# A four-layer fp32 block on one core: nine weight slots and one used once, layers that open with the high part of x, and other waits at their openings

## What is computed

```python
x = x + rmsnorm(even_mixer(rmsnorm(x)))   # attention of 16 heads beside a state-space model
x = x + rmsnorm(odd_mixer(rmsnorm(x)))    # pooling at four scales, gates, two projections
for layer in range(2):
    h = h + hybrid_mixer(rms_norm(h))     # retention of 4 heads beside a gated recurrence of 4 heads
    h = h + expert_choice_ffn(rms_norm(h))
# expert_choice_ffn: softmax over 16 experts; each expert takes its 32 best tokens (top_k),
# silu(xe @ w_gate) * (xe @ w_up) @ w_down, all [1024, 1024], scattered back with the gates
return rms_norm(h)
```

## Time and profile before

| | |
|---|---|
| three runs | 1701.05, 1702.65, 1705.38 us, median 1702.65 |
| the profiled execution | 1701.89 us, its span 1700.1 us |
| PE, PEld busy | 1330.2 us (78%), 931.5 us (55%) |
| DVE, ACT, POOL busy | 558.6, 433.6, 139.2 us |
| transfers | 517.22 MB, 304 GB/s over the span |
| the chain that ended last | 45% transfers, 39% PE, 6% DVE, 3% SP's queue |

### The profile page before, as it was taken

How to read it: one execution, slowest core, us unless ns; L and a number is a source line. 1 busy time by engine, 2 the same in 40 slices (tenths; PEclk the granted TensorE clock), 3 DMA queues, 4 the chain that set the end, 5 groups by cost and what they waited for, 6 DMA issues and landing times.

```text
span 1700.1 us, 28164 instructions
## 1 busy us (share of the span) xinstructions
PE 1330.2 (78%) x12488; PEld 931.5 (55%) x12488; DVE 558.6 (33%) x804; ACT 433.6 (26%) x570; POOL 139.2 (8%) x155
## 2 busy tenths in 40 slices
PE   7999989999899987656556665999977666666564
PEld 5688867998798844323222322788843333233232
DVE  7854775455566530000000001485520000000001
ACT  5236335443554311100101001454311101001011
POOL 0130300000304000000000000304000000000000
PEclk9999999999999979888888888999989878879887
DMA  9134333464444699999999999344799999999996
GB/s 327 51 120 154 112 136 143 154 221 171 142 156 174 255 387 425 424 426 423 426 424 425 425 425 411 125 149 174 301 403 423 426 424 425 425 423 426 423 425 263
DMA packets 86216, 517.22 MB, mean 304 GB/s; under 512 B 6352, under 2 KB 6480, under 8 KB 53072
## 3 DMA queue, kind: packets, MB, share of 16 engines
q1 hardware_dynamic: 82592, 509.20, 73.8%
q0 software_dynamic: 992, 3.42, 0.6%
q10 hardware_dynamic: 2512, 2.75, 0.5%
HBM read 514.30 MB, written 1.05 MB: 303 GB/s over the span
## 4 chain that ended last, share of the span: by engine, by line
DMA 45%; PE 39%; DVE 6%; SPq 3%; POOL 2%; ACT 2%; issue 2%; DVEq 0%; ACTq 0%; POOLq 0%
DMA ring<-in_w_down 15%; DMA ring<-in_w_up 14%; PE dense L1562 8%; PE dense L1564 8%; PE dense L1563 8%; DMA ring<-in_w_gate 7%; DMA board<-in_w_up 5%; PE bank L2073 3%; SPq L608 3%; DMA board<-in_w_down 2%; PE dense L1579 2%; DMA ring<-in_even_w_in 2%; PE bank L2098 1%; DVE ring_parts L1211 1%; ACT ring_parts L832 1%
## 5 line engine op out<-in xcount | busy, mean ns | idle before, releaser
L2073 PE MATMUL bank<-ring,board 128*32 128x256 f32 x2432 | 194.7, 474 | 144.0 <-DMA ring<-in_w_up 68.1
L2073 PEld LDWEIGHTS bank<-ring,board 128*32 128x32 f32 x2432 | 90.6, 131 | 242.1 <-DMA ring<-in_w_up 84.8
L1211 DVE TENSOR_TENSOR ring_parts<-ring,ring_parts 128x4096 fp32r<-128x4096 f32 (+1 forms) x44 | 183.8, 4187 | 110.7 <-ACT ring_parts L832 110.6
L1004 ACT ACTIVATE board<-bank 128x256 f32<-128x256 f32 x32 | 12.3, 384 | 751.9 <-PE bank L2073 751.9
L1482 DVE TENSOR_TENSOR board<-board,bank 128x256 f32<-128x256 f32 x32 | 13.5, 422 | 562.2 <-ACT board L1004 562.2
L832 ACT ACTIVATE ring_parts<-ring 128x4096 fp32r<-128x4096 f32 (+1 forms) x45 | 154.1, 3432 | 100.8 <-DMA ring<-in_w_in 43.9
L2073 PE MATMUL bank<-board 128*32 128x256 f32 x1664 | 118.9, 435 | 67.7 <-DMA board<-in_w_up 46.1
L1562 PE MATMUL dense<-board_parts,ring_parts 128*128 128x256 f32 x528 | 152.2, 288 | 3.1 <-DVE ring_parts L1211 3.1
L1562 PE MATMUL dense<-ring_parts,board_parts 128*128 128x512 f32 x352 | 143.3, 407 | 8.5 <-ACT board L757 2.3
L1564 PE MATMUL dense<-board_parts,ring_parts 128*128 128x256 f32 x528 | 149.4, 283 | 0.0
L1563 PE MATMUL dense<-ring_parts,board_parts 128*128 128x512 f32 x352 | 138.8, 394 | 0.0
(11 more groups left out here) (330 smaller groups left out, 2036.5 us busy)
## 6 DMA issues: line engine op xcount, KB each, us to landing
ring<-in_w_gate SPq DMA_DIRECT2D x38, 2048.0 KB, 42.0
ring<-in_w_up SPq DMA_DIRECT2D x38, 2048.0 KB, 42.1
ring<-in_w_down SPq DMA_DIRECT2D x38, 2048.0 KB, 41.6
board<-in_w_gate SPq DMA_DIRECT2D x26, 2048.0 KB, 42.4
board<-in_w_up SPq DMA_DIRECT2D x26, 2048.0 KB, 41.0
board<-in_w_down SPq DMA_DIRECT2D x26, 2048.0 KB, 42.1
ring<-in_w_in SPq DMA_DIRECT2D x18, 2048.0 KB, 8.0
ring<-in_even_w_in SPq DMA_DIRECT2D x10, 2048.0 KB, 10.3
```

The source lines that it names most:

```text
L1211: tt(lo, slot_of(u), hi.bitcast(F32), ALU.subtract).then_inc(lo_done, 1)
L2073: last = mm(WB[0][32 * q:32 * q + 32, 256 * (j % 2):256 * (j % 2) + 256], xeT[:, 4 * (j // 2) + k, :], w[:, k * D + 256 * q:k * D + 256 * ...
```

## The change

Line numbers here and in the lists are those of the changed kernel where a list says so.

1. **Slots.** Expert units turn through nine slots. The tenth (`ONCE`) takes unit 9 of each expert layer and nothing more. The experts' loop has a head of two (`HEAD_E`), four turns of three, and two behind it. The loads of the first ten units of a layer wait for what they waited for before.
2. **High parts of 11, 12, 13** are made by ACT, between the exponentials, not by POOL.
3. **Openings of layers 2 and 3** (`opening_unit`): for each tile, PE issues high x times both parts of w as soon as each half of high x is there, then waits for low x and issues its products, then transposes the second tile. The parts of the second unit (`SECOND`, 15 and 31) are made in halves (ACT, `high_half`) and quarters (DVE) inside `norm_between`.
4. **Opening of layer 4**: PE waits for x by halves (`full_half`); DVE makes the low part of unit 138 before it multiplies the second tile by the gain.
5. **Waits**: `ret_transposes(w)` waits for its own four rotations; the first output unit waits for `DO + 10`, takes tile 1 first and waits for `DO + 11` in its middle.
6. **Zero matmuls**: 128x512 zeros; one round of four as before, and three rounds more (twelve matmuls) behind the affinities' transposes. DVE writes the zeros later.
7. **Ends**: the last expert unit of a layer comes in four transfers of 512 KB, awaited one by one; the last scatter goes by accumulators and releases DVE's first addition after four of eight; the output is scaled and sent in halves, four transfers of 256 KB.

```diff
-WHEEL = RING + EXTRA
-TURN_E = 5
-
-EXTRA_OF = {2: 2, 3: 1, 4: 0, 9: 3}
+WHEEL = RING + EXTRA - 1
+TURN_E = 3
+
+
+ONCE = WHEEL
+HEAD_E = 2
+EXTRA_OF = {2: 2, 3: 1, 4: 0}
+
+
+def wheel_place(j):
+
+    return j if j < ONCE else (j - ONCE - 1) % WHEEL
+
+
+def extra_slot(j):
+
+    return EXTRA - 1 if j == ONCE else EXTRA_OF.get(wheel_place(j))
...
-                    elif j >= WHEEL:
-                        sp.wait_ge(unit_done, u - WHEEL + 1)
+                    elif j > ONCE:
+                        sp.wait_ge(unit_done, u - (WHEEL if j - ONCE > WHEEL else WHEEL + 1) + 1)
...
+                    elif turn is None and e == NE - 1 and j == 5:
+
+                        for n in range(4):
+                            src = down[e, :, 2 + n // 2, n % 2, :]
+                            dst = slot_mem(s)[:, n * FF:(n + 1) * FF]
+                            sp.dma_start(dst, src).then_inc(tail_in[n - 1] if n else landed[s], 16)
+                        return
                     else:
...
                 sum_rms(0)
                 dense_rms(1)
                 gain_high(0, at)
+                high_half(SECOND[k - 1], 0)
                 sum_rms(1)
+                high_half(SECOND[k - 1], 1)
...
+            def high_half(u, half):
+
+                if half == 0:
+                    act.wait_ge(landed[slot_no[u]], 16 * count_in[u])
+                    act.wait_ge(unit_done, free_at(high_place[u]))
+                k = slice(4 * half, 4 * half + 4)
+                s.activation(slot_of(u, True)[0][:, k], slot_of(u)[:, k], ACT.Copy).then_inc((hi_half, hi_done)[half], 1)
...
             exps(3)
             t_out(9, gaT, 0, ACT.Silu)
+            high_part(11)
             exps(4)
             t_out(10, gaT, 4, ACT.Silu)
-            for n in (5, 6, 7):
-                exps(n)
+            high_part(12)
+            exps(5)
+            exps(6)
+            high_part(13)
+            exps(7)
             high_part(14)
             norm_between(13, 1)
-            high_part(15)
             for g in range(4):
                 high_part(16 + g)
                 tok_out(14 + g, u_tok, 512 * g)
...
                         tt(x[:, i, half], x[:, i, half], xs[:, i, half], ALU.add).then_inc((sum_half, x_ready)[b], 1)
+                    if i:
+                        low_part(SECOND[k - 1], 0)
                     dve.wait_ge(x_ready, 2 * (k - 1) + i + 1)
                     dve.wait_ge(sum_half, 2 * (k - 1) + i + 1)
                     normalise(i)
+                    if i:
+                        low_part(SECOND[k - 1], 1)
                     gain_out(i, name, x_lo if k == 1 else x_lo2)
+                low_part(SECOND[k - 1], 2)
+                low_part(SECOND[k - 1], 3)
 
...
-                tt(zeros, ident, ident, ALU.subtract).then_inc(zero_set, 1)
                 add_half(0, 0)
                 add_half(0, 1)
                 dve.wait_ge(half_ps, 6 + 2 * l)
                 add_half(1, 0)
                 gain_out(0, f"n2_{l}")
+                tt(zeros, con[:, 0:512], con[:, 0:512], ALU.subtract).then_inc(zero_set, 1)
                 normalise(0)
                 dve.wait_ge(unit_done, MOE[l])
...
-                dve.wait_ge(sc_y, NE * (l + 1))
                 for i in range(NT):
                     for b in range(2):
+                        dve.wait_ge(*((sc_y, NE * (l + 1)) if i + b else (sc_first, l + 1)))
...
                         dve.wait_ge(x_ready, 8 + 2 * i)
                         normalise(i)
+                        if i:
+                            low_part(FIRST2[1] + 1)
                         for half in range(2):
...
-                stt(xs[:, i, :], x[:, i, :], rstd[:, i:i + 1], row[:], ALU.mult, ALU.mult).then_inc(final_done, 1)
+                for b in range(2):
+                    half = slice(512 * b, 512 * b + 512)
+                    stt(xs[:, i, half], x[:, i, half], rstd[:, i:i + 1], row[:, half], ALU.mult,
+                        ALU.mult).then_inc(final_done, 1)
...
+            def opening_unit(u, low, d, hi_at):
+
+
+                w = slot_of(u, True)
+                arrived(u)
+                for i in range(NT):
+                    rows = slice(i * P, (i + 1) * P)
+                    for half in range(2):
+                        pe.wait_ge(gain_hi, hi_at + 2 * i + half + 1)
+                        for k in range(4 * half, 4 * half + 4):
+                            mm(d[:, i, :], xT_r[:, k, rows], w[0][:, k, :], start=k == 0, stop=False)
+                            mm(d[:, i, :], xT_r[:, k, rows], w[1][:, k, :], start=False, stop=False)
+                    tile_in_xT()
+                    for k in range(DC):
+                        last = mm(d[:, i, :], low[:, k, i, :], w[0][:, k, :], start=False, stop=k == DC - 1)
+                    if i == 0:
+                        transpose_x(1)
                 last.then_inc(unit_done, 1)
 
...
-            tile_in_xT()
...
-                token_unit(14 + g, (xT_r, x_lo), DP[g % 2], [[], [at(pooled, g - 1)], [], []] if g else
-                           [[], [at(transpose_x, 1)], [tile_in_xT], []])
+                if g == 0:
+                    opening_unit(14, x_lo, DP[0], 0)
+                else:
+                    token_unit(14 + g, (xT_r, x_lo), DP[g % 2], [[], [at(pooled, g - 1)], [], []])
...
+                def full_half():
+
+                    count["full"] += 1
+                    pe.wait_ge(full_ready, count["full"])
+
                 transpose_x(0)
-                (full_rows if l else tile_in_xT)()
 
...
-                    pe.wait_ge(rot_done, 8 * (l + 1))
+                    pe.wait_ge(rot_done, 8 * l + 4 * (w + 1))
...
-                ahead_of[0] = [[], [at(transpose_x, 1)], [full_rows if l else tile_in_xT], []]
+                ahead_of[0] = [[full_half], [full_half, at(transpose_x, 1)], [full_rows], []]
...
-                pe.wait_ge(dense_out, DO + 11)
+                def bank_read():
+                    pe.wait_ge(dense_out, DO + 11)
+
+
+                pe.wait_ge(dense_out, DO + 10)
                 pe.wait_ge(router_in, 32)
                 for n in range(2):
                     pe.wait_ge(gm_sb, 4 * l + 2 * (n + 1))
                     chunks = range(4 - 4 * n, 8 - 4 * n)
                     rows_unit(OUT2[l] + n, [[t[:, c, :] for c in chunks] for t in (m_hi, m_lo)], n == 0, n == 1,
-                              [[], [], [at(mix_transposes, 0)], []] if n == 0 else [[], [], [], [first_rows]],
-                              [[], [], [], [first_logits]] if n else ())
+                              [[], [], [bank_read, at(mix_transposes, 0)], []] if n == 0 else [[], [], [], [first_rows]],
...
-                for r in range(4):
-                    last = mm(yb[r], zeros, m_hi[:, 0:2, :].rearrange("p c s -> p (c s)"), start=True, stop=True)
-                    if r >= 2:
-                        last.then_inc((ge_ps, gt_ps)[r - 2], 1)
+
+                def zero(rounds):
+
+                    for _ in range(rounds):
+                        for r in range(4):
+                            last = mm(yb[r], zeros[:, 0:P], zeros, start=True, stop=True)
+                    return last
+
+                zero(1).then_inc(ge_ps, 1)
                 pe.wait_ge(aff_sb, l + 1)
                 for i in range(NT):
                     last = tr(WB[1][0:NE, i * P:(i + 1) * P], aff[:, i, :], ident)
                 last.then_inc(aff_ps, 1)
+                zero(3).then_inc(gt_ps, 1)
 
...
+                                if not more and j == 1 and qq + b > 0:
+                                    pe.wait_ge(tail_in[2 * qq + b - 1], 16 * (l + 1))
...
-                    for i in range(NT):
-                        for r in range(4):
-                            rows = slice(32 * r, 32 * r + 32)
-                            last = mm(yb[r][:, 256 * i:256 * i + 256], wselT[rows, i, :], ye[rows, :], start=False,
-                                      stop=False, skip_group_check=True)
+                    for i, r in product(range(NT), range(4)) if more else ((i, r) for r, i in product(range(4), range(NT))):
+                        rows = slice(32 * r, 32 * r + 32)
+                        last = mm(yb[r][:, 256 * i:256 * i + 256], wselT[rows, i, :], ye[rows, :], start=False,
+                                  stop=False, skip_group_check=True)
+                        if not more and (i, r) == (1, 1):
+                            last.then_inc(sc_first, 1)
```

70 lines of the change are left out of this document (38 added, 32 removed).

## The result

The changed kernel takes 1677.79 us (median of four runs, 1676.85 to 1680.37) against 1704.02 for the kernel before on the same chip: ratio 0.9854, 95% interval 0.9836 to 0.9873. Of 1703 us that is 24.9 us, between 21.6 and 27.9. I had forecast 16.3. Its profiled execution has a span of 1676.5, 23.6 less than before.

The account below looks back on a forecast made before the run. The prediction took a chain of mixers and two transfer-bound expert streams as the bound. Its terms summed to -16.3 us, from 1701.89 to 1685.6 in the profiled execution, 1686.4 on the median, range 1680 to 1695.

Parts of the forecast that it names:

- A stream of fixed length: Expert layers 3 and 4: transfers at 424 and 425 GB/s set the time; savings inside a stream gain nothing.
- nine slots: 0: Expert streams: one slot fewer shortens the queue of transfers, not their rate; 0 us.
- Attention -5.2: Attention: high parts moved from POOL to ACT free short DVE operations and shorten PE's waits; -5.2 us, span nothing to 6.0.
- rival 2: Openings of layers 2, 3 and 4: the clock falls in the new short pauses; 1689.1 us, chance 0.10.
- Openings -1.9 and -3.0: Openings of layers 2 and 3: PE starts earlier and waits less for low parts; -1.9 and -3.0 us.
- Waits -3.1: Waits for rotations in two layers, -2.9 us, and the finer wait for the gates, -0.2 us.
- Zero matmuls -1.7: Routing wait: twelve more zero matmuls keep the clock up for layer 3's first expert; -1.7 us, nothing for layer 4.
- Opening of layer 4 +1.7: Opening of layer 4: second tile starts later behind unit 138's low part, perhaps at half clock; +1.7 us.
- the transfer does not move: Opening of layer 4: ACT's copy for unit 138 waits for a transfer taken as fixed, so starts at 1065.55 as before.
- End -3.1: End of program: last unit in quarters -2.0, scatter order -0.6, output by halves -0.5; together -3.1 us.
- rival 1: Attention: ScalarE becomes what is waited for, DVE's product waiting for exponentials; 1690.0 us, chance 0.12.
- rivals 3 to 5: 3: waits only move, 1695, 0.05; 4: gains don't reach end, 1699.5, 0.03; 5: nine slots throttle transfers, 1710 to 1780, 0.05.

Follow-up runs that it names:

- x2: Changed kernel with its nine slots but turns of six experts instead of three: 1681.0 us, ratio 0.9878 to the kernel before.
- x3: Kernel before with only the changed kernel's nine slots, head of two and turns of three: 1697.4 us, ratio 0.9970 to the kernel before.
- y3: Changed kernel with the old openings of layers 2 and 3 put back: 1685.1 us, ratio 0.9891 to the kernel before.
- y1: Kernel before with only ScalarE, not POOL, making the high parts of units 11 to 13: 1696.4 us, ratio 0.9958 to the kernel before.
- y2: Changed kernel with the low part of unit 138 moved back behind the split of x: 1671.8 us, ratio 0.9813 to the kernel before.
- w2: Changed kernel with unit 138's low part back behind the split of x and one round of zero matmuls: 1675.2 us, ratio 0.9823 to the kernel before.
- z1: Changed kernel with the old waits for rotations and for the output unit: 1677.7 us, ratio 0.9861 to the kernel before.
- x1: Changed kernel with ten slots, turns of five and no head, as before: 1685.7 us, ratio 0.9909 to the kernel before.
- y4: Changed kernel with one round of zero matmuls, none behind the affinities' transposes: 1677.3 us, ratio 0.9850 to the kernel before.
- z2: Changed kernel with eight experts ahead of the loop instead of two: 1679.9 us, ratio 0.9875 to the kernel before.
- x4: Changed kernel with each layer's last expert unit in one 2 MB transfer again: 1681.5 us, ratio 0.9876 to the kernel before.

## Why the prediction missed

The time fell 2.2 us under its range. By its own steps:

- **"A stream of fixed length" and "nine slots: 0"** is the step that failed: two streams are 3.2 us shorter each in the profiles, 6.4 together. I looked at what the slots do to the queue, which was right as far as x2 can tell (nine slots with a long turn: no gain clear of the spread), and never asked what the turn of three does to the code. The rows were there: PE's waits under "issue" of 5.8 us in the loop, and an instruction queue in the transfers. The Trainium skill, page "Advanced Engine Details and Errata", section "ISA Cache", gives lines of 16 KB or 256 instructions, and 128 KB of them on TensorE. By this case's rows (below) an expert is some 457 instructions of PE: 3114 matmuls and 3104 weight loads in 400 us, which is 13.6 experts of 29.4 us. Three are 1,370, five 2,280, six 2,740. An estimate from the page's figures is that 8 lines, 2,048 instructions, fit, so that a turn of three is held and turns of five or six aren't. The trace agrees with the size of a line (0.46 MB in 28 packets are 16 KB each) and roughly with the number: by the page's line, the 12.9 experts of 380 us, fetched anew, are an estimated 12.9 x 457 / 256 = 23 packets, and the rows have 25 to 28. How much is held no run here measured, only that a turn of three was not fetched anew and turns of five and six were; nor do the rows say which engine's code a packet carries. The changed kernel, from 640 to 1040 (columns as in rows 1):

```profile
640.00:1040.00 400.00, 247.90 (x3114) 116.74 (x3104) 25.88 (x70) 33.95 (x59) 9.84 (x26) 0.87 1.01 425
```

- **Attention -5.2**: measured 6.7 in the trace and 7.2 in time. The waits were sized nearly right (4.9); the half clock behind the longest of them, which was in my own rows, was left out of the sum. x3 shows it too, at the same place. The rule of the Trainium skill that I set beside the trace in rival 2, page "TensorE: Matmul & The Clock Gate", section "HAM oscillation — how this bites in real kernels", that waits between groups of matmuls throttle the engine, speaks for this change as much as against it: the wait of 3.0 that went had 0.52 behind it.
- **Openings -1.9 and -3.0**: measured together 6.9 between the two traces (2.6 and 4.3), and 6.3 by y3. The second again has a clock in it: 5.9 us at half clock before (431.4 to 437.3), 3.5 after. That is 1.2 of the 1.3 missing. Other profiles bear it out: with the old openings (before, x3, y1, y3) the clock is near half for 6.8 us in all in the second one, with the new ones for 3.4, or not at all (y2, w2). And the 1.00 behind the wait of 3.1, which I held against rival 2, was one execution's: in x3, y1 and y3 the same wait, 3.1 us long, has half clock behind it. This is y1, whose wait ends at 442.14 (columns as in rows 1):

```profile
442.20:445.50 3.30, 3.30 (x16) 3.30 (x17) 3.30 (x1) 0.00 (x0) 3.30 (x1) 0.51 1.05 404
```

- **Waits -3.1**: 3.3 by z1's trace, all of it at the rotations, where I had 2.9. The 0.2 for the output unit isn't seen.
- **Zero matmuls -1.7**: nothing. The mechanism fell: I took one execution's clock for a property of the kernel.
- **Opening of layer 4 +1.7**, between 0.8 and 2.6: from the last landing of layer 3 to unit 138 28.3 against 27.3 us, so +1.0 in this pair of traces. The mechanism is as written, DVE and PE wait for the copy, and the second tile is slow as in the upper bound; but "the transfer does not move" was wrong, it landed 1.5 us sooner behind the last unit, as it did in x3 and y1 with the old opening, so not by this change. In x1, y4, z1 and z2, whose second tile ran at full clock, the same stretch takes 26.5 to 26.7, less than before: there the loss that I forecast is none.
- **End -3.1**: 14.4 to 11.1 is -3.3, and the match is luck in part. The quarters gave 1.3, not 2.0. About 1.6 is clock (the scatter takes 1.17 against 2.09), which no part of the change is shown to give. x3 has the end of the kernel before and takes 12.8 us, with its scatter in 1.15, while y1, with the same end, takes 14.5. That leaves 0.4 for the order of the scatter and the halves of the output (x3 against x4), where I had 1.1.

Together -6.4 - 6.7 - 6.9 - 3.3 + 1.0 - 3.3 = -25.6. The spans differ by 23.6 and the starts by 2.1 the other way, so by 25.7 from the same instruction on; the ratio gives 24.9. Of the 9.3 us between -25.6 and my sum of -16.3 the streams are 6.4. Attention and openings gave 3.5 more than I said, about 2.9 of it clock behind waits that the change took away; the waits and the end gave 0.4 more, the opening of layer 4 took 0.7 less, and the zeros gave 1.7 less. Neither rival 1 nor rivals 3 to 5 occurred.

**Still open**: how 20 packets, 0.4% of the engines' share and so 1.7 us of 430, come to 3.2. Part is seen at the very end of the second stream, where the transfers run at about half rate before they stop: five us of it in the kernel before, two in the changed one, whose rows stand in this order:

```profile
1679.00:1684.00 5.00, 2.98 (x36) 1.58 (x36) 0.42 (x1) 2.60 (x5) 0.00 (x0) 0.90 0.52 215
```

```profile
1662.00:1664.00 2.00, 1.60 (x32) 0.56 (x22) 0.00 (x0) 0.23 (x2) 0.00 (x0) 1.00 0.43 170
```

The same twelve us ahead of the last landing, read in steps of one us, sort all fourteen profiles: under 300 GB/s for 7 or 8 of them in the four with long turns (before, x1, x2, y1), for 3 to 5 in the nine with turns of three, for 6 in z2. What is missing there against 425 GB/s is 4.3 us of transfers in the kernel before and 2.8 in the changed one. With the 1.7 that makes an estimate of 3.2, the size of the gain; the end of the first stream can't be read so, since the next layer's loads run on behind it. Why the rate falls at the end is not shown. Some of the 16 DMA engines having work left when the others are done would do it, and instruction packets on a few of them would make it worse; which engine carries what, these profiles don't show.
